# Where the matmuls' operands start in SBUF: another layout of activation parts and weight parts

## What is computed

```python
h = rms_norm(x, attn_norm[l]);  proj = h @ w_in[l]
y_ret  = o_r @ w_ret_o[l];      y_moba = o_m @ w_moba_o[l]
gates = jax.nn.sigmoid(h @ w_gate[l] + b_gate[l])
x = x + (gate_ret * y_ret + gate_moba * y_moba) @ w_out[l]
h = rms_norm(x, ffn_norm[l]);   u = causal_depthwise_conv(h @ w_up[l], conv_w[l], conv_b[l])
x = x + (jax.nn.silu(u_gate) * u_val) @ w_down[l]
```

## The kernel before

| part | before | after |
|---|---|---|
| `h_hi`, `h_lo` | 32, 32 | 0, 32 |
| `a_hi`, `a_lo` | 32, 32 | 64, 16 |
| weights of slot 0, high and low | 32, 32 moving; 0, 0 stationary | 0, 32 |
| slot 1 | the same | 64, 96 |
| slot 2 | the same | 16, 48 |
| slot 3 | the same | 8, 80 |
| `area` (tables, q, k, v of the attention) | 64 | 0 |
| `ys`, `ident` | 0, 0 | 64, 64 |

## Time and profile before

### The profile page before, as it was taken

How to read it: one execution, slowest core, us unless ns; L and a number is a source line. 1 busy time by engine, 2 the same in 40 slices (tenths; PEclk the granted TensorE clock), 3 DMA queues, 4 the chain that set the end, 5 groups by cost and what they waited for, 6 DMA issues and landing times.

```text
span 450.2 us, 6345 instructions
## 1 busy us (share of the span) xinstructions
PE 446.6 (99%) x2477; PEld 390.5 (87%) x2477; DVE 337.6 (75%) x395; ACT 286.3 (64%) x384; POOL 102.6 (23%) x69
## 2 busy tenths in 40 slices
PE   9999999999999999999999999999999999999997
PEld 6899988888888999999999888888888888888886
DVE  4789994876699839673368578589999999987423
ACT  6885453055996759233425368499999999996300
POOL 0100021499360021210000003333433333300000
PEclk9999999999999999999999999999999999999999
DMA  8997658557999425997555553977787778873102
GB/s 278 422 406 255 251 190 234 141 186 204 258 268 310 177 94 181 278 317 254 188 188 190 184 187 113 318 247 234 233 242 233 239 245 243 252 250 128 58 0 93
DMA packets 61385, 98.70 MB, mean 219 GB/s; under 512 B 48048, under 2 KB 48944, under 8 KB 52016
## 3 DMA queue, kind: packets, MB, share of 16 engines
q1 hardware_dynamic: 60944, 96.79, 67.6%
q0 software_dynamic: 416, 1.57, 1.0%
HBM read 85.77 MB, written 1.05 MB: 193 GB/s over the span
## 4 chain that ended last, share of the span: by engine, by line
PE 99%; DVE 0%; issue 0%; POOL 0%; POOLq 0%
PE bank L558 8%; PE bank L560 8%; PE bank L559 8%; PE bank L751 8%; PE bank L750 8%; PE bank L749 8%; PE bank L511 6%; PE bank L512 6%; PE bank L510 6%; PE bank L796 4%; PE bank L794 4%; PE bank L793 4%; PE bank L697 2%; PE bank L696 2%; PE bank L695 2%; PE bank L524 2%
## 5 line engine op out<-in xcount | busy, mean ns | idle before, releaser
L1079 DVE TENSOR_TENSOR w_pair<-w_raw,w_pair 128x2048 fp32r<-128x2048 f32 x73 | 176.4, 2437 | 47.2 <-ACT w_pair L813 46.9
L813 ACT ACTIVATE w_pair<-w_raw 128x2048 fp32r<-128x2048 f32 x73 | 139.0, 1924 | 30.9 <-PE bank L560 13.3
L749 PE MATMUL bank<-w_pair,h_hi 128*128 128x512 f32 x160 | 62.2, 389 | 0.0
L750 PE MATMUL bank<-w_pair,h_hi 128*128 128x512 f32 x160 | 62.2, 389 | 0.0
L751 PE MATMUL bank<-w_pair,h_lo 128*128 128x512 f32 x160 | 62.2, 389 | 0.0
L558 PE MATMUL bank<-a_hi,w_pair 128*128 128x256 f32 x192 | 53.8, 280 | 0.0
L559 PE MATMUL bank<-a_lo,w_pair 128*128 128x256 f32 x192 | 53.6, 279 | 0.0
L560 PE MATMUL bank<-a_hi,w_pair 128*128 128x256 f32 x192 | 53.6, 279 | 0.0
L510 PE MATMUL bank<-w_pair,h_hi 128*128 128x512 f32 x128 | 49.9, 390 | 0.0
L511 PE MATMUL bank<-w_pair,h_hi 128*128 128x512 f32 x128 | 49.8, 389 | 0.0
L512 PE MATMUL bank<-w_pair,h_lo 128*128 128x512 f32 x128 | 49.8, 389 | 0.0
(11 more groups left out here) (162 smaller groups left out, 853.6 us busy)
## 6 DMA issues: line engine op xcount, KB each, us to landing
w_raw<-weights_dram SPq DMA_DIRECT2D x73, 1024.0 KB, 5.8
w_raw<-weights_dram SPq DMA_DIRECT2D x8, 256.0 KB, 5.2
w_raw<-weights_dram SPq DMA_DIRECT2D x4, 512.0 KB, 8.8
ys<-x_dram SPq DMA_DIRECT2D x2, 512.0 KB, 8.9
xs<-x_dram POOLq DMA_DIRECT2D x1, 1024.0 KB, 5.4
area<-decay_dram SPq DMA_DIRECT2D x1, 768.0 KB, 8.8
out_dram<-ys SPq DMA_DIRECT2D x3, 256.0 KB, 2.0
xs<-x_chan_dram SPq DMA_DIRECT2D x1, 512.0 KB, 6.7
```

The lines of the kernel that those rows point to most:

```text
L749: mm(o, s_hi, hi[:, kk, :], start=(k == 0), stop=False)
L750: mm(o, s_hi, lo[:, kk, :], start=False, stop=False)
L813: A(w_parts(n, r)[0], raw[r][:, :], ACT.Copy).then_inc(hi_ready, 1)
L1079: tt(lo, raw[r][:, :], hi.bitcast(f32), ALU.subtract).then_inc(lo_ready, 1)
```

## The change

The switch between two positions of a weight part by role (`SHIFT`, 8 elements, for weights that are moving) goes. Each slot has fixed positions for its high and low part instead, from `PART_COLUMNS`, the same whether the weights are moving or stationary. The activation parts and small tensors are declared in another order, and `a_lo` starts 4 elements into its tensor, so that the starts are those of the table above. Two spare tensors of 32 bytes fill gaps. The instructions and their order on every engine are the same.

```diff
--- before.py
+++ after.py
@@ -18,7 +18,7 @@
 BLOCK_COLS = 512
 HALF_ELEMS = 2048
 SLOTS = 4
-SHIFT = 8
+PART_COLUMNS = ((0, HALF_ELEMS + 8), (0, HALF_ELEMS + 8), (4, HALF_ELEMS + 12), (2, HALF_ELEMS + 20))
 UP_COLS = 256
 UP_BLOCKS = D_FF // UP_COLS
 DOWN_HALVES = D_FF // P // 2
@@ -73,29 +73,35 @@
 
 
         raw = [sb(f"w_raw{r}", [P, HALF_ELEMS]) for r in range(SLOTS)]
+
+        def by_k(name, tiles, first=0):
+            whole = sb(name, [P, first + tiles * SEQ], f32r)
+            return whole[:, first:first + tiles * SEQ].rearrange("p (k s) -> p k s", k=tiles)
+
+        h_hi = by_k("h_hi", KT)
         inv_x = sb("inv_x", [P, 2])
-        h_hi = sb("h_hi", [P, KT, SEQ], f32r)
-        h_lo = sb("h_lo", [P, KT, SEQ], f32r)
-
-        a_hi = sb("a_hi", [P, D_FF // P, SEQ], f32r)
-        a_lo = sb("a_lo", [P, D_FF // P, SEQ], f32r)
+        h_lo = by_k("h_lo", KT)
+        ss_x = sb("ss_x", [P, 2])
+        a_hi = by_k("a_hi", D_FF // P)
+        gn_rstd = sb("gn_rstd", [P, 8])
+        ss_x2 = sb("ss_x2", [P, 4])
+        a_lo = by_k("a_lo", D_FF // P, 4)
         gn_stats = sb("gn_stats", [P, 8, 6])
-        ss_x = sb("ss_x", [P, 2])
-        w_pair0 = sb("w_pair0", [P, SHIFT + 2 * HALF_ELEMS], f32r)
+        inv_x2 = sb("inv_x2", [P, 2])
+        w_pair0 = sb("w_pair0", [P, 2 * HALF_ELEMS + 8], f32r)
+        neg_half = sb("neg_half", [P, 8])
+        w_pair1 = sb("w_pair1", [P, 2 * HALF_ELEMS + 8], f32r)
+        spare = sb("spare", [P, 8])
+        w_pair2 = sb("w_pair2", [P, 2 * HALF_ELEMS + 16], f32r)
+        row_max = sb("row_max", [P, 16])
+        w_pair3 = sb("w_pair3", [P, 2 * HALF_ELEMS + 24], f32r)
         ss_qk = sb("ss_qk", [P, 4, 8])
-        row_max = sb("row_max", [P, 16])
-        gn_rstd = sb("gn_rstd", [P, 8])
-        w_pair1 = sb("w_pair1", [P, SHIFT + 2 * HALF_ELEMS], f32r)
         inv_qk = sb("inv_qk", [P, 4, 8])
         neg_max = sb("neg_max", [P, 16])
-        neg_half = sb("neg_half", [P, 8])
-        w_pair2 = sb("w_pair2", [P, SHIFT + 2 * HALF_ELEMS], f32r)
         row_sum = sb("row_sum", [P, 16])
         inv_sum = sb("inv_sum", [P, 16])
         gn_mv = sb("gn_mv", [P, 8, 2])
-        ss_x2 = sb("ss_x2", [P, 4])
-        w_pair3 = sb("w_pair3", [P, SHIFT + 2 * HALF_ELEMS], f32r)
-        inv_x2 = sb("inv_x2", [P, 2])
+        spare2 = sb("spare2", [P, 8])
         area = sb("area", [P, 8192])
         x_head = sb("xs", [P, 2 * KT + 2048])
         w_pair = [w_pair0, w_pair1, w_pair2, w_pair3]
@@ -270,9 +276,7 @@
         def w_parts(n, r=None):
 
             r = n % SLOTS if r is None else r
-            moving = not isinstance(n, int) or n // 2 in TOKEN_BLOCKS or n >= 2 * UP0
-            first = SHIFT if moving else 0
-            return [w_pair[r][:, first + HALF_ELEMS * i:first + HALF_ELEMS * i + HALF_ELEMS] for i in range(2)]
+            return [w_pair[r][:, c:c + HALF_ELEMS] for c in PART_COLUMNS[r]]
 
         block = ctx.enter_context(nc.Block())
```

## The result

The changed kernel takes 460.82 us (median of 460.67 and 460.97) against 452.48 us: +8.3 us, a ratio of 1.0188 with a 95% interval of 1.017 to 1.0207. The profiled execution has a span of 458.8 us against 450.2.

What follows compares the result with a forecast made beforehand. TensorE was taken as the bound, busy 446.6 of 450.2 us. Stationary term -1.0, moving starts on multiples of 64 +3.8, other moving starts +2.9 give +5.7 us on 452.5, so 458.2 us, range 447 to 467.

Steps and rivals of the forecast that it cites:

- Nothing on the other engines: ACT and DVE lines writing the split parts: no price for their new starts, staying near 1920 and 2290 ns.
- The cover on DVE: Up-projection, 119 us: DVE busy 110.2, so 8.8 us spare; it must be 8% slower before it shows.
- The stationary term: All matmuls: a stationary start off a multiple of 64 costs 8 columns, 3.33 ns; 300 fewer pay it, -1.0 us.
- The moving term: All matmuls: 8 columns more for moving starts not at 32 or 96; +3.8 us on multiples of 64, +2.9 us elsewhere.
- My reason for its size: Matmul intervals: on top is 32 columns plus the stationary start's 4-byte elements past its line, minus the moving start's.
- The classes named as a test: Up-projection and channel blocks: intervals fall into classes by slot; slot 0 hi x hi 226.7 ns, most channel classes at least 120.
- The condition for being wrong: Odd starts costing far more than a step, a long PE wait for DVE, or same-class intervals differing by what preceded.
- (b): Matmuls: the moving start doesn't matter, only the stationary one; -1.0 us, 451.5 us; chance 0.18.
- (c): Matmuls: moving start, like the stationary, 8 columns cheaper on a multiple of 64; -4.8 us, 447.7 us; chance 0.11.
- (d): Matmuls: start difference counts round a circle of 32 columns, 128 bytes; -10.4 us, 442.1 us; chance 0.04.
- Rival (a): Matmuls: a moving start away from 32 costs 16 columns, not 8; +12.4 us, 464.9 us; chance 0.27.
- my steps: Each matmul: summed prices, 8 columns for a stationary start off a multiple of 64, 8 for moving not at 32 or 96.

Runs made afterwards that it cites:

- the streams: Kernels with the layer left out, TensorE alone running float32r matmuls at chosen start pairs; at 512 columns, 32 with 32 settled at 226.7 ns, 128 with 32 at 234.4.
- first streams: TensorE alone, layer left out, 16 matmuls per stream, 64 start pairs, then alternating starts; of 56 unequal pairs at 512 columns, 47 lay between 40 and 52 columns on top.
- the control: Kernel before with only the small tensors between the parts in another order, all parts at their old starts modulo 256: 452.31 us, ratio 1.0002.
- streams of 48: TensorE alone, layer left out, streams lengthened from 16 to 48 matmuls; at 512 columns 0 with 0 ran at 226.7 ns, 0 with 32 at 234.4.

## Why the prediction was right, and where it was not

The forecast was 458.2 us, +5.7; measured are 460.8, +8.3, inside the range and on the forecast side. But that is luck in good part: in the two kinds of matmuls the forecast was 6.5 us too low and 3.7 us too high, and the two errors cancel in part.

- **What bounds it** held: 99% PE before and after, and the difference of the matmul intervals (8.5 us) is the difference of the spans.
- **Nothing on the other engines** held: L817 and L1083 at 1916 and 2292 ns. The cover on DVE was never needed.
- **The stationary term** (-1.0 us, with -3.0 in the token blocks) failed. It took the 3.3 ns between the earlier trace rows for the price of a stationary start off a multiple of 64. The two rows differ in the pair, 128 with 160 against 160 with 160 past a multiple of 256, and the price goes by the pair: in the streams at 512 columns, a stationary start at 128 in place of 32 costs 7.7 ns beside a moving start at 32 and saves 6.6 beside one at 128. And stationary weights at 224, off a multiple of 64, gave 116.3 ns where the step says 120.0.
- **The moving term** (+6.7 us) has the right sign and the wrong form. Moving weights at 0 beside activations at 32 took 16 columns more, not 8 (+10.3 us, forecast +4.5), and four slots moved by 128 bytes took +8.7 us where the step says 0. For starts at 8, 16, 48 and 80 I had 8 columns; the streams with equal starts there are 11 to 16 columns above 32 with 32. My reason for its size, a difference of starts that fitted both rows, fitted two numbers with one constant and a rule; it was no evidence.
- **The split** shows it (intervals from a matmul's start to the next one's): forecast +0.8 us in the 512-column matmuls and +4.9 in the 256-column ones, measured +7.3 and +1.2. The classes named as a test came out against me: in slot 0 of the changed kernel 0 with 0 is at 231.7 ns (forecast 226.7), h_hi with 32 at 233.7 (223.3), h_lo with 0 at 228.5 (230). Of the channel blocks' classes that I set at or above 120 ns, one is there (122.0, slot 3 high with a_hi), the others are below.
- **The condition for being wrong**, that intervals of one class differ by what ran before them, is met (113.2 and 117.7 ns in one slot of the run with stationary weights at 224).
- **Rivals (b), (c) and (d)** forecast a faster kernel (-1.0, -4.8 and -10.4 us), and the sign refutes them. In (d) the mean on top before is 28.8 columns, not 28.5; it changes that sum by 0.1 us.

What the runs put in its place: a stream of float32r matmuls with one constant pair of starts mostly settles into a rhythm. At 512 columns that is 32 on top where both operands start at the same multiple of 32 past a multiple of 256 bytes (160 with 160 in the kernel before, 128 with 128 in the run with all parts at 0, 32, 64, 96 and 128 in the streams), and 45 to 48 on top in the layer where constant starts differ. The change takes this equality from all token blocks and gets 42 to 49 on top by slot and stage. The 256-column blocks had no equal pair before and lose little. Rival (a), a larger step for the moving start, had the step that the run with moving weights at 0 measured, 16 columns, but not the mechanism. The Trainium skill, page "TensorE: Matmul & The Clock Gate", has no start address in the N/2.4 + 2.5 ns of its section "Back-to-back issue gap" (which that section calls the gap of an isolated matmul, not of a stream with weight loads), and its section "Step-by-step: what each phase is for" says that loading the next weights takes no SBUF read bandwidth from the running matmul. That the change is therefore worth nothing, as I read the two, does not hold for this type: 226.7, 232.4 and 233.3 ns are measured for the same 512 columns. Whether it is the reads that get in each other's way no run here shows.

Here is how the additive steps and the runs compare, in us over the kernel before:

| run | my steps | measured | 512 columns, ns | 256 columns, ns |
|---|---|---|---|---|
| changed kernel | +5.7 | +8.3 | 232.15 | 117.9 |
| weight positions alone | +6.0 | +8.8 | 232.0 | 118.6 |
| activation positions alone | -0.2 | +7.8 | 232.0 | 117.5 |
| weights at 0 | +4.5 | +10.3 | 233.3 | 118.3 |
| all at 0 | +3.2 | +3.1 | 226.8 | 120.0 |
| stationary weights at 32 | +3.2 | +6.7 | 230.4 | 119.4 |
| stationary weights at 96 | +3.2 | +3.3 | 230.4 | 115.3 |
| slots 128 further | 0 | +8.7 | 232.4 | 118.0 |
| stationary at 224 | +3.2 | +0.3 | 226.8 | 116.3 |
| stationary at 48 | +3.2 | +2.8 | 226.9 | 119.8 |

What stays open: why the rhythm goes by 256 bytes, why six of 56 unequal pairs ran at 32 on top in the first streams (so equal starts are not the only cheap ones, at least in a short stream), and what decides between two rhythms of one pair. Each kernel of streams ran once. If all channel halves could be held at 113.3 ns in place of 116.7, that would be 960 x 3.4 ns, 3.3 us, my estimate from the two figures; no run here did it. The runs show when it happens, not which part of the memory or the array makes the wait. Nor do they show how much of the changed kernel's +7.3 us comes from unequal pairs and how much from starts that change within a block; constant unequal pairs alone give as much.

## What to carry to other kernels

In a kernel that is bound by streams of float32r matmuls, place the stationary and the moving operand of a 512-column stream at the same distance, a multiple of 32, past a multiple of 256 bytes, and keep it so for high and low parts alike; it was worth about 2% here (8.3 to 10.3 us of 452). Check the addresses of the built program modulo 256 whenever a small tensor is added or a buffer grows, since 128 bytes on four buffers cost as much as the whole change. And before two rows are turned into a price for each operand, find a third that has one of the two alone: two rows that differ in a pair can't tell a sum from an interaction.

## What was not expected of the hardware

- A move of four buffers by 128 bytes costs 8.6 us of 452 against the control, with no other difference.
- A stream can need some intervals to settle (230, 236, 228, 234, 230 ns, then 226.7); in the streams of 48 with 0 with 0 or 32 with 32 it took none to nine.
- At 256 columns equal starts, best at 512, are among the dear ones (120.0 ns), and 128 with 64 settles at 113.3 ns; but the same distance in the layer (224 with 160) ran at 113.2 ns in one half and 117.7 in another of one run, and switched there only where the stream had been broken.
